# Two halves of the tokens summed one after the other, in place of alternating, in the products of a two-layer encoder

## The reference, cut to what matters

```python
def sq_relu_mlp(h, w_up, w_down):
    return jnp.square(jax.nn.relu(h @ w_up)) @ w_down

# layer 0: qkv_a, z_a, b_a, a_a, q_b, k_b, v_b, f_b = split(rmsnorm(x) @ w_in)
#          gated DeltaNet heads and forgetting attention; concat(...) @ w_out
# layer 1: q, k, v = split(rmsnorm(x) @ w_in); window attention; o @ w_out
# both:    mk, mv = split(rmsnorm(mem, g) @ w_kv)
#          x = x + cross_attend(rmsnorm(x), mk, mv, wq, wo)
#          x = x + sq_relu_mlp(rmsnorm(x), w_up, w_down)
```

## Time and profile before

| | |
|---|---|
| three runs | 1831.49, 1832.55, 1837.18 us |
| median | 1832.55 us |
| profiled execution, first to last instruction (span) | 1822.3 us |
| median less span | 10.2 us |
| TensorE matmul (PE) busy | 1715.4 us, 94% |
| weight load (PEld) busy | 1612.7 us, 88% |
| VectorE (DVE) busy | 798.1 us, 44% |
| ScalarE (ACT) busy | 623.2 us, 34% |
| GpSimd (POOL) busy | 511.3 us, 28% |

### The profile page before, as it was taken

The page is one execution under the profiler, slowest core; times in us unless marked ns, Lnnn a source line. Parts: engine busy times, 40 slices in busy tenths (PEclk is TensorE's granted clock), DMA queues, the critical chain, the costliest instruction groups (busy, mean ns, idle before and its releaser), DMA issues.

```text
span 1822.3 us, 30662 instructions
## 1 busy us (share of the span) xinstructions
PE 1715.4 (94%) x12758; PEld 1612.7 (88%) x12758; DVE 798.1 (44%) x1561; ACT 623.2 (34%) x1188; POOL 511.3 (28%) x158
## 2 busy tenths in 40 slices
PE   6999788899998889999999999899989999999998
PEld 5999756888788789999999999557988999999998
DVE  4129773554257462222222541675645422222235
ACT  4113372222144343131312331775334422222232
POOL 3533300000025213443344433001441343334331
PEclk9999998999599999999999999889999999999999
DMA  4223200000043202222222224000330222222221
GB/s 145 73 90 94 94 25 6 1 1 1 12 139 116 93 24 93 83 80 93 92 92 76 85 93 145 31 1 9 107 118 24 74 89 93 93 92 80 82 92 49
DMA packets 123015, 131.32 MB, mean 72 GB/s; under 512 B 6269, under 2 KB 115106, under 8 KB 122914
## 3 DMA queue, kind: packets, MB, share of 16 engines
q1 hardware_dynamic: 116898, 123.37, 20.7%
q10 hardware_dynamic: 6016, 6.54, 1.1%
HBM read 122.44 MB, written 7.45 MB: 71 GB/s over the span
## 4 chain that ended last, share of the span: by engine, by line
PE 86%; DVE 8%; ACT 3%; issue 2%; SPq 0%; DMA 0%; ACTq 0%; DVEq 0%
PE LP L649 66%; PE LP L959 5%; PE MP L765 3%; PE LP L731 3%; PE MP L749 2%; DVE acc L1652 1%; DVE xl L1659 1%; PE LP L881 1%; PE MP L1037 1%; PE MP L1036 1%; PE MP L1029 1%; DVE probs L1718 1%; PE MP L1024 0%; DVE nm L1723 0%; ACT wh L1195 0%
## 5 line engine op out<-in xcount | busy, mean ns | idle before, releaser
L577 POOL TENSOR_TENSOR wl<-stage,wh 128x2048 fp32r<-128x2048 f32 x108 | 498.0, 4612 | 1275.4 <-ACT wh L1195 1275.3
L649 PE MATMUL LP<-xh,wh 128*128 128x272 f32 x2176 | 457.0, 291 | 13.0 <-DVE xl L1659 5.2
L649 PE MATMUL LP<-xh,wl 128*128 128x272 f32 x2176 | 452.6, 290 | 0.0
L649 PE MATMUL LP<-xl,wh 128*128 128x272 f32 x2176 | 451.5, 289 | 0.0
L1195 ACT CAST wh<-stage 128x2048 fp32r<-128x2048 f32 x108 | 205.6, 1904 | 475.2 <-PE LP L649 463.4
L649 PEld LDWEIGHTS LP<-xh,wh 128*128 128x128 f32 x2176 | 344.4, 190 | 17.5 <-DVE xl L1659 7.1
L649 PEld LDWEIGHTS LP<-xl,wh 128*128 128x128 f32 x2176 | 344.9, 190 | 0.0
L649 PEld LDWEIGHTS LP<-xh,wl 128*128 128x128 f32 x2176 | 342.4, 190 | 0.0
L649 PE MATMUL LP<-hh,wh 128*128 128x272 f32 x1024 | 211.2, 287 | 0.0
L649 PE MATMUL LP<-hh,wl 128*128 128x272 f32 x1024 | 210.6, 288 | 0.0
L649 PE MATMUL LP<-hl,wh 128*128 128x272 f32 x1024 | 210.3, 287 | 0.0
(11 more groups left out here) (309 smaller groups left out, 2055.6 us busy)
## 6 DMA issues: line engine op xcount, KB each, us to landing
stage<-in_w_up SPq DMA_DIRECT2D x32, 1024.0 KB, 5.3
stage<-in_w_down SPq DMA_DIRECT2D x32, 1024.0 KB, 5.0
stage<-in_w_in_ab SPq DMA_DIRECT2D x13, 1024.0 KB, 5.1
stage<-in_w_xkv SPq DMA_DIRECT2D x8, 1024.0 KB, 5.1
stage<-in_w_in_c SPq DMA_DIRECT2D x6, 1024.0 KB, 4.8
stage<-in_w_out_ab SPq DMA_DIRECT2D x4, 1024.0 KB, 7.2
stage<-in_w_xq SPq DMA_DIRECT2D x4, 1024.0 KB, 5.3
stage<-in_w_xo SPq DMA_DIRECT2D x4, 1024.0 KB, 5.9
```

The costliest lines, as they stand in the source:

```text
L577: pool.tensor_tensor(wl[s][:, :], stage[s][:, :], wh[s][:, :].bitcast(f32), ALU.subtract).then_inc(w_lo, 1)
L649: mm = pe.matmul(LP[:, 2 * slot + half, 0:b - a], weights, X[part][:, k, a:b], start=(first and n_ == 0), stop=(last and n_ == 2), skip_gr ...
```

## The change

In the tiles that are issued one after the other, the loop over `k` runs for half 0 of the tokens and then again for half 1. A new argument `which` tells `block` which halves to issue, and `product_done` is raised only when the last half is among them. The staggered tiles are issued as before, and a product of one piece has only one half.

```diff
--- before.py
+++ after.py
@@ -641,14 +641,15 @@
         def _(pe):
             TOKENS = ((0, HALF), (HALF, N))
 
-            def block(slot, s, col, k, first, last, kt, halves, X):
+            def block(slot, s, col, k, first, last, kt, halves, X, which=None):
 
                 for n_, (w, part) in enumerate(((wh, 0), (wh, 1), (wl, 0))):
                     weights = w[s][:, :].rearrange("p (k n) -> p k n", k=kt)[:, k, col:col + 128]
                     for half, (a, b) in enumerate(halves):
-                        mm = pe.matmul(LP[:, 2 * slot + half, 0:b - a], weights, X[part][:, k, a:b],
-                                       start=(first and n_ == 0), stop=(last and n_ == 2), skip_group_check=True)
-                if last:
+                        if which is None or half in which:
+                            mm = pe.matmul(LP[:, 2 * slot + half, 0:b - a], weights, X[part][:, k, a:b],
+                                           start=(first and n_ == 0), stop=(last and n_ == 2), skip_group_check=True)
+                if last and (which is None or len(halves) - 1 in which):
                     mm.then_inc(product_done, 1)
 
             def pair(free, Pn, tpp, kt, halves, X, ready, after_first=None, order=None, between=None):
@@ -680,8 +681,9 @@
                     for i in range(2 if s == 0 and ready is not None else 0, tpp):
                         tile_n = s * tpp + i
                         wait_free(tile_n)
-                        for k in range(kt):
-                            block(tile_n % 2, s, 128 * i, k, k == 0, k == kt - 1, kt, halves, X)
+                        for half in range(len(halves)):
+                            for k in range(kt):
+                                block(tile_n % 2, s, 128 * i, k, k == 0, k == kt - 1, kt, halves, X, (half,))
 
             def reads(signal, base):
```

## The result

The changed kernel took 1834.87 us in the median of 20 runs (1830.14 to 1846.08), the kernel before 1831.71 us in 20 runs (1824.53 to 1837.18). The ratio is 1.0027, with a 95% interval of 1.0014 to 1.0039: slower by 0.27%, some 4.9 us (2.6 to 7.1); the two medians alone are 3.2 us apart. That is within the 0.3% that the prediction called no difference, but it is not zero. The forecast was 1833.8 us, +1.2 us.

The account below looks back on a forecast made before the run. The prediction took TensorE's steady matmul pace as the bound: 1822.3 us of span plus 10.2 us around it is the median, 1832.5; with +1.2 us for 8160 moved matmuls it forecast 1833.8 us, range 1829 to 1841.

Parts of the forecast that it names:

- the 0.3% that the prediction called no difference: Whole kernel: about 0.3%, 5.5 us, is what a measurement can tell from no change; no difference to be seen got 0.83.
- What bounds the kernel: Whole span: TensorE's matmuls, busy 94%, go at their own pace, so the distance from one matmul to the next matters.
- The 10.2 us: Around the profiled span: 10.2 us added to 1822.3 us of span to give the median, 1832.5 us.
- The 8160 moved matmuls, no wait and no signal moved: 178 product tiles: 8160 matmuls change order; a tile's first wait and its `product_done` stay, other engines see the old times.
- The price of a moved matmul: Each of 8160 moved matmuls: bank and weights together cost 0.15 ns (-0.2 to +0.8), +1.2 us in all.
- the memory product: Product of the memory tokens, 256 columns, one half, already in the new order: 118.7 ns a matmul, used to price the change.
- surplus: Steady product matmuls at 2.4 GHz: time beyond the columns alone, 11.7 ns at 272 columns; all that order could change.
- the 0.3 ns: Per moved matmul: 12.0 ns at 256 columns in one bank less 11.7 ns at 272, read as cost of bank and weights.
- The two readings: Distance between product matmuls before: 124.7 ns from seven 40 us MLP stretches, 125.3 ns from 31 timeline pairs; 125.0 taken.
- The slower rival: Every moved matmul: weight changes or returning to the bank just written cost 0.8 to 1.2 ns, about 1841 us; chance 0.09.
- The faster rival: Moved matmuls: the surplus comes from alternating banks and goes; half gives 1785 us, all 1737 us; chance 0.04.
- The clock rival: Products: 12 us of half clock enter or leave them, giving 1826 or 1840 us; chance 0.02 to each side.

## Why the prediction was right or wrong

**What bounds the kernel:** right. All of the difference is in the distance between products' matmuls; waits, counts and the other engines stayed, as foreseen. The 10.2 us that the sum puts around the span are not there: in the runs of the kernel before that list both, time and span are 1.7 to 3.6 us apart. The rest of the 10.2 is that the profiled execution was one of the faster ones, with a clock of 0.961; it cancels in the sum.

**The 8160 moved matmuls, no wait and no signal moved:** right. The staggered tiles, the tile's wait and `product_done` show nothing new.

**The price of a moved matmul** (+0.15 ns taken, -0.2 to +0.8 given): this is the step that was mis-sized, and its reason was wrong. Over all 8160 the 4.9 us are 0.6 ns each, four times the value taken. In one block the two products lose 0.33 and 0.20 us on 672 moved matmuls, 0.79 ns each, at the upper bound. In a layer's MLP that makes four times 0.33, three times 0.20 and the first block's 288 at 0.5 ns, 2.1 us. The stretch of 3264 matmuls that also holds the output of the cross attention took 413.9 us before, from 1393.4, and 416.0 after, from 1398.5. That is 4.2 us for both layers. Elsewhere 54 tiles of `xh` and `xl` moved (input, output and query products); at 0.20 us for eight, as in the MLP, they cost at most 1.4 us, and less where they wait or run at a lower clock. The 16 tiles of the cross attention's output (24 matmuls each) moved too and cost nothing: 3.01 us each before and after. So the distances give up to 5.6 us. That fits the 4.9 (2.6 to 7.1) by the ratio and lies somewhat above what equal clock gives, 4.2 (3.3 to 5.0). That the forecast still held is in part luck: the price of a moved matmul was four times the one in the sum, and its cause another.

The price had been taken from the memory product, on the premise that a surplus belongs to the order and not to the width or the place. At 256 columns the old order turned out to be slower than the new one: h 45.72 against 45.56. And the 0.3 ns were a difference between arrays from the start. The two readings, 124.7 and 125.3 ns, were not two readings of one thing, as the prediction took them: the seven stretches mix both products of the MLP, the timeline lies in a first product alone. The first product goes at 48.11 / 384 = 125.3 ns, a surplus of 12.0, and the second at 124.5, a surplus of 11.1. The memory product's 12.0 is that of the first product to the tenth, so by its own method the prediction would have had a price of nothing for `xh` and `xl`, where 0.5 ns were measured, and one of 0.9 ns for `hh` and `hl`, where 1.1 were.

**The slower rival** had the sign right and, in the MLP, the size at which it begins (0.67 ns; measured 0.79 there, 0.6 over all), and both its mechanisms wrong. More changes of weights cost nothing (h 47.80, x 48.11 with 4 in 6), and one bank cost nothing (47.81 and 48.11 with 24 in a row). What costs is the sequence of places that the inputs are read from: that is shown by leaving out the others and by the kernels that change the places alone; how it costs is not. So the outcome lay at the edge between two cases of which neither named its cause.

**The rule of the Trainium skill** (TensorE: Matmul & The Clock Gate, "Step-by-step: what each phase is for"), load once and multiply repeatedly, was rightly set aside for this kernel: with the halves alternating, more neighbours with the same weights gained nothing, 47.80 us with 2 changes in 6 and with 4. The Trainium skill (same page, same section) also says that the next weights load while a matmul runs. The trace agrees: weight loads are busy for 88% of a span of which matmuls fill 94%, so the two overlap.

**The faster rival** was wrong: banks alternating or not, the surplus stays (47.80 and 47.81 us, 11.1 ns). Its cause is open; over all kernels at 272 columns it is 11.0 to 13.3 ns (x time 47.74 to 48.64 us, 124.3 to 126.7 ns a matmul).

**The clock rival** was not the cause of the difference, but it is the largest scatter. The profile after shows it at the window attention (length, busy and count of PE, PEld, DVE, ACT and POOL, clock, DMA):

```profile
1125.00:1170.00 45.00, 41.71 (x212) 30.72 (x210) 16.82 (x64) 19.37 (x61) 9.10 (x2) 0.74 0.36 123
```

0.74 there, where the kernel before had 0.81 in its profiled execution. It does so from run to run in both kernels: the kernel before's own granted clocks went from 0.949 to 0.962 and its spans from 1821.4 to 1843.2 us.

**What stays open:** by which rule addresses and sequence set the distance, and what else chooses between the paces that one stream can have. The gaps moved the weights, and all that lies behind them, against `xh` together with `xl`, so which operands matter is not told apart. Whether the more frequent changes of weights cost something in the new order was not tried either; with the halves alternating they did not. A version with 128 bytes between `xh` and `xl`, the new order in the products of `x` and the old one in those of `h`, would by these times gain 0.37 us in each first product of the MLP (48.11 to 47.74) and lose 0.16 us per eight tiles in the input product of layer 0 (48.11 to 48.27); that is an estimate and holds only if each stream settles at the same pace again. It was not run, nor was the old order with that gap.

## What to carry to other kernels

When a stream of matmuls runs without waits, measure it by the start of one product to the start of the next over a known count: here that repeats to 0.02 us in 48 for one product of one kernel, and tells 0.05 ns a matmul, while the whole kernel's time scatters by 1% with the clock. A difference of half a nanosecond between two such streams belongs to their arrays' addresses and widths as much as to their order, so the price of a new order is not to be taken from another product. Nor is one product enough: read several that use the same arrays, since 384 matmuls took 48.27 us in one and 47.73 in another of the same kernel. And spans are compared at equal granted clock when the effect is a few tenths of a percent.

## What the runs showed of the hardware that was not expected

The distance between matmuls of 128x272 at 2.4 GHz depended on where the inputs lie and in which sequence they are read: 124.3 ns (new order, gap of 128 bytes) to 126.7 ns (new order, half 0 read twice) for the same products of `xh` and `xl`. It did not depend on the bank written (h 47.81 us with 24 in a row in one bank, 47.80 alternating; in the new order 48.13 and 48.14) nor, with the halves alternating, on how often the weights change (47.80 with 2 and with 4 changes in 6). Within one kernel, the same arrays in the same order went at 125.7 ns in one product and 124.3 in another, and an interruption inside a product could move the stream from one steady pace to another (6.03 to 6.05 us a tile). And a gap of 128 bytes in front of `hh` left the old order as it was and changed the new one by 0.05 us.
